# RWKV-7 recurrence stage: triangular inverse over four array quarters, half-width levels, state work moved into later levels

## What is computed

```python
def step(S, inp):                       # S: 64 x 64 per head
    r_t, w_t, k_t, v_t, a_t, b_t = inp
    sa = einsum('bhij,bhj->bhi', S, a_t)
    S = S * w_t[:, :, None, :] + sa[..., None] * b_t[:, :, None, :] + v_t[..., None] * k_t[:, :, None, :]
    return S, einsum('bhij,bhj->bhi', S, r_t)
S, ys = lax.scan(step, S0, xs)          # over 1024 tokens
```

## Time and profile before

| | us |
|---|---|
| median of 3 runs (1789.14 to 1791.79) | 1790.33 |
| the profiled execution's own time | 1789.6 |
| its span | 1787.8 |
| the recurrence stage in it, first activity to the store of the last state | about 468 to 732 |
| TensorE busy in the whole span | 1539.6 |
| VectorE busy | 668.1 |
| ScalarE busy | 371.5 |
| GpSimd busy | 211.5 |

### The profile page before, as it was taken

The page is one execution under the profiler, slowest core; times in us unless marked ns, Lnnn a source line. Parts: engine busy times, 40 slices in busy tenths (PEclk is TensorE's granted clock), DMA queues, the critical chain, the costliest instruction groups (busy, mean ns, idle before and its releaser), DMA issues. The chain is left out here.

```text
span 1787.8 us, 29869 instructions
## 1 busy us (share of the span) xinstructions
PE 1539.6 (86%) x11901; PEld 965.6 (54%) x11902; DVE 668.1 (37%) x1128; ACT 371.5 (21%) x813; POOL 211.5 (12%) x271
## 2 busy tenths in 40 slices
PE   7999999666899999546996699999499489999968
PEld 4666666454788888422442344444379344444433
DVE  1122560177255455481334311111478611111117
ACT  1232100266222322210001111111122111111111
POOL 3000000000322221210000111000500011110030
PEclk8999999877799999877998799999679789999989
DMA  6671110121000000005115688788501587867543
GB/s 178 151 306 48 26 46 0 39 67 25 2 4 4 4 4 4 8 0 156 36 38 185 241 287 294 279 283 261 202 22 61 177 289 275 304 240 254 188 172 148
DMA packets 138477, 237.23 MB, mean 133 GB/s; under 512 B 21570, under 2 KB 101427, under 8 KB 138090
## 3 DMA queue, kind: packets, MB, share of 16 engines
q1 hardware_dynamic: 114834, 151.01, 26.7%
q0 software_dynamic: 16912, 60.52, 9.2%
q10 hardware_dynamic: 6624, 24.12, 3.3%
HBM read 178.95 MB, written 58.21 MB: 133 GB/s over the span
## 5 line engine op out<-in xcount | busy, mean ns | idle before, releaser
L2094 PE MATMUL ex_pb<-ew_w_gate_up,ex_xT 128*128 x736 | 329.3, 601 | 6.1 <-DVE ex_xT L2139 2.3
L298 PE MATMUL pj_pb<-pj_xT,pj_w 128*128 128x348 f32 (+3 forms) x960 | 284.2, 457 | 0.4 <-ACT pj_xT L322 0.4
L298 PEld LDWEIGHTS pj_pb<-pj_xT,pj_w 128*128 128x128 f32 (+1 forms) x960 | 179.7, 187 | 102.7 <-issue 2.7
L2094 PEld LDWEIGHTS ex_pb<-ew_w_gate_up,ex_xT 128*128 128x128 f32 x736 | 137.7, 192 | 164.8 <-issue 163.8
L2077 PE MATMUL ex_pb<-ew_w_down,ex_hiddenT 128*128 x368 | 165.7, 593 | 3.4 <-ACT ex_hiddenT L2164 3.4
L2287 DVE TENSOR_TENSOR ex_hidden<-ex_hidden,ex_pb 128x256 f32<-128x256 f32 x46 | 19.4, 421 | 324.0 <-ACT ex_hidden L2159 324.0
L2077 PEld LDWEIGHTS ex_pb<-ew_w_down,ex_hiddenT 128*128 128x128 f32 x368 | 66.3, 190 | 69.9 <-issue 69.9
L1826 PE MATMUL mo_pb<-mo_w,minus_kk_then_y 128*128 128x512 f32 (+1 forms) x144 | 66.6, 617 | 20.8 <-DMA mo_w<-in_w_out 20.8
L2282 DVE COPY ex_y_rows<-ex_pb 128x512 f32<-128x512 f32 x46 | 31.8, 692 | 134.5 <-PE ex_pb L2077 134.5
L430 DVE SCALAR_TENSOR_TENSOR mixed<-pj_pb,v_mu,mixed 128x347 f32<-128x347 f32 (+3 forms) x42 | 24.0, 572 | 147.8 <-ACT mixed L372 147.7
L1826 PE MATMUL mo_pb<-mo_w,projected_qkv 128*128 128x512 f32 (+1 forms) x144 | 66.1, 614 | 7.3 <-DMA mo_w<-in_w_out 7.3
(11 more groups left out here) (428 smaller groups left out, 2292.6 us busy)
## 6 DMA issues: line engine op xcount, KB each, us to landing
ew_w_gate_up<-in_w_ex_gate SPq DMA_DIRECT2D x32, 1024.0 KB, 7.8
ew_w_gate_up<-in_w_ex_up SPq DMA_DIRECT2D x32, 1024.0 KB, 10.5
ew_w_down<-in_w_ex_down SPq DMA_DIRECT2D x32, 1024.0 KB, 13.1
scratch_slots_out<-ex_y_rows ACTq DMA_DIRECT2D x46, 512.0 KB, 5.2
scratch_slots_out<-pj_tmp POOLq DMA_DIRECT2D x4, 4096.0 KB, 15.9
scratch_x_stored<-x_rows SPq DMA_DIRECT2D x16, 512.0 KB
pj_w<-in_w_in SPq DMA_DIRECT2D x7, 1024.0 KB, 9.5
minus_kk_then_y<-in_x_prompt SPq DMA_DIRECT2D x8, 512.0 KB, 5.5
```

What stands on the lines that cost most here:

```text
L298: last = nc.tensor.matmul(product(at)[:, 0:tn], w[:, s % NW, k, c0:c0 + mrows], xT[:, k, x0:x0 + tn], start=(k == 0), stop=(k == KD - 1))
L2094: last = mm(pb[:, 2 + u, :], xT[:, u, k, :], w[:, k, :], start=(k == 0), stop=(k == KD - 1))
```

## The change

It rewrites `rwkv_chunks` and the masks it needs. What is computed, the tiles, the chunks and the number of levels stay.

- Quarters: for odd heads X (not XT) and Z live on the other half of the partitions (`to = fr(ch ^ par)`), and each group of products goes t, par, ch in turn, so that consecutive matmuls fall in all four quarters. The level products go to banks 6 and 7 (both Z and X), the transposes to 0 and 1.
- The product with r, the keys by a, and the output too go over four quarters; the output is now 32 matmuls of 64 x 64 instead of 16 of 128 x 128 columns.
- Both triangles (b a^T and a b^T) are made by TensorE (`triangles`), 32 matmuls instead of 16, so that XT of level 0 is masked directly; the GpSimd step that made X (L1052) and the VectorE step of L1270 fall away, and one VectorE step adds the identity.
- Half-width levels: a level changes only half of the columns, so Z, the addition to XT, the transposes of levels 1 to 4 and the copies of X use 32 columns per matrix.
- VectorE and ScalarE take both parities in one instruction.
- XT and RT have two buffers. The triangles of tile n+1 are made at the end of tile n, before the product with the values.
- State work of tile n-1 is spread over the levels of tile n: `state_by_w` at levels 0 and 2, `state_terms` after them, `state_update` in levels 1 and 3, `output` in level 4.
- RT holds only the diagonal blocks; the memset of RT at the start falls away.

TensorE's new parts and order:

```diff
+            def triangles(n):
+                pe.wait_ge(q["ft"], 2 * n + 1)
+                if n:
+                    pe.wait_ge(q["xc"], NLEV * n)
+                for t in range(4):
+                    for at, lhs, rhs in ((0, B, A), (256, A, B)):
+                        for par in range(2):
+                            for ch in range(2):
+                                cc = slice(P * n + CH * ch, P * n + CH * ch + CH)
+                                last = mm(pb[fr(ch), par, at + CH * t:at + CH * t + CH], lhs[fr(par), t, cc],
+                                          rhs[fr(par), t, cc], start=True, stop=True)
...
+            def transposed(n, lev):
...
+                                last = mm(grouped(pb[to, par, P * t:P * t + HALF], lev - 1), XT[cc, n % 2, par, t, :],
+                                          half_of(ident[cc, cc], lev - 1, 0), start=True, stop=True)
...
+            def level_z(n, lev):
+                if lev:
+                    pe.wait_ge(q["xe"], NLEV * n + lev)
+                    if n and lev in (1, 3):
+                        pe.wait_ge(q["uc"], 2 * (n - 1) + (lev + 1) // 2)
...
+                for t in range(4):
+                    for par in range(2):
+                        for ch in range(2):
+                            cc, to = fr(ch), fr(ch ^ par)
+                            last = mm(grouped(pb[to, 6 + par, P * t:P * t + HALF], lev), Lm[cc, par, t, :],
+                                      half_of(XT[cc, n % 2, par, t, :], lev, 1), start=True, stop=True)
+                last.then_inc(q["z"], 1)
+            def level_x(n, lev):
+                pe.wait_ge(q["zc"], NLEV * n + lev + 1)
+                if n and lev in (0, 2):
+                    state_by_w(n - 1, lev // 2)
+                pe.wait_ge(q["xc"], NLEV * n + lev + 1)
+                for t in range(4):
+                    for par in range(2):
+                        for ch in range(2):
+                            cc, to = fr(ch ^ par), fr(ch)
+                            last = mm(pb[to, 6 + par, P * t:P * t + HALF], X[cc, par, t, :], Z[cc, par, t, :],
+                                      start=True, stop=True)
...
+            triangles(0)
+            for n in range(NT):
+                transposed(n, 0)
+                level_z(n, 0)
+                by_r(n)
+                level_x(n, 0)
+                if n:
+                    state_terms(n - 1, 0)
+                level_z(n, 1)
+                transposed(n, 1)
+                if n:
+                    state_update(n - 1, 0)
+                keys_by_a(n)
+                level_x(n, 1)
+                level_z(n, 2)
+                transposed(n, 2)
+                level_x(n, 2)
+                if n:
+                    state_terms(n - 1, 1)
+                level_z(n, 3)
+                transposed(n, 3)
+                if n:
+                    state_update(n - 1, 1)
+                token_rows(n, 0)
+                level_x(n, 3)
+                token_rows(n, 1)
+                level_z(n, 4)
+                transposed(n, 4)
+                if n:
+                    output(n - 1)
+                token_rows(n, 2)
+                level_x(n, 4)
+                token_rows(n, 3)
+                if n + 1 < NT:
+                    triangles(n + 1)
+                values(n)
+                inverse_applied(n)
```

VectorE's order, and the widths of its steps:

```diff
+                tt(xt, up, four("lev0T"), ALU.mult).then_inc(q["x0"], 1)
+                dve.wait_ge(q["x0"], n + 1)
+                tt(flat(xt), flat(xt), eight("eye"), ALU.add).then_inc(q["xe0"], 1)
+                tt(Lm[:, :, :, :], low, four("low"), ALU.mult).then_inc(q["lc"], 1)
...
+            def take_z(n, lev):
+                dve.wait_ge(q["z"], NLEV * n + lev + 1)
+                tt(flat(Z[:, :, :, :]), level_out(6), eight(f"lev{lev + 1}T"), ALU.mult).then_inc(q["zc"], 1)
+            def take_x(n, lev):
+                dve.wait_ge(q["x"], NLEV * n + lev + 1)
+                new = halves_of(XT[:, n % 2, :, :, :], lev, 1)
+                tt(new, new, level_out_grouped(6, lev), ALU.add).then_inc(q["xe"], 1)
...
+            for n in range(NT):
+                take_triangles(n)
+                take_z(n, 0)
+                take_by_r(n, 0)
+                take_by_r(n, 1)
+                take_x(n, 0)
+                if n:
+                    take_u(n - 1, 0)
+                take_z(n, 1)
+                if n:
+                    take_state(n - 1, 0)
+                take_x(n, 1)
+                take_z(n, 2)
+                take_keys(n)
+                take_x(n, 2)
+                if n:
+                    take_u(n - 1, 1)
+                take_z(n, 3)
+                if n:
+                    take_state(n - 1, 1)
+                take_x(n, 3)
+                take_z(n, 4)
+                take_x(n, 4)
```

More of the change, by code:

```diff
@@ L1044, in scaled @@
                 last.then_inc(q["hat"], 1)
-            for z in (ST[:, 0, :, :], RT[:, :, :, :, :]):
-                nc.gpsimd.memset(z, 0.0).then_inc(q["start"], 1)
-            scaled(0)
+            nc.gpsimd.memset(ST[:, 0, :, :], 0.0).then_inc(q["start"], 1)
             for n in range(NT):
[L1051 to L1055, removed]
+                scaled(n)
         @block.tensor
@@ new lines, in level_x @@
+            def level_x(n, lev):
[3 more added lines that the diff above has]
+                pe.wait_ge(q["xc"], NLEV * n + lev + 1)
+                for t in range(4):
+                    for par in range(2):
+                        for ch in range(2):
+                            cc, to = fr(ch ^ par), fr(ch)
+                            last = mm(pb[to, 6 + par, P * t:P * t + HALF], X[cc, par, t, :], Z[cc, par, t, :],
+                                      start=True, stop=True)
+                last.then_inc(q["x"], 1)
@@ new lines, in token_rows @@
+            def token_rows(n, j):
+                src = (bh[:, :, :], kh[:, :, :], A[:, :, tile_cols(n)], pr[:, 8:12, tile_cols(n)])[j]
+                if j < 2:
+                    pe.wait_ge(q["mc"], n + 1)
+                    if n and j:
+                        pe.wait_ge(q["sc"], 2 * n)
+                    pe.wait_ge(q["hat"], n + 1)
+                else:
+                    pe.wait_ge(q["tc"], 4 * n + j - 1)
+                for t in range(4):
+                    last = nc.tensor.transpose(pb[:, 4 + j % 2, P * t:P * t + P], src[:, t, :], ident[:, :])
+                last.then_inc(q["tr"], 1)
@@ L1118, in output @@
             def output(n):
+                pe.wait_ge(q["sc"], 2 * n + 2)
                 for t in range(4):
-                    for par in range(2):
-                        hc = hcol(par, t)
-                        o = pb[fr(par), 3, P * t:P * t + P]
-                        mm(o, U[:, hc:hc + HD], RT[:, par, 0, t, :], start=False, stop=False)
-                        last = mm(o, tok[:, 3, hc:hc + HD], RT[:, par, 1, t, :], start=False, stop=(t == 3))
-                last.then_inc(q["y"], 1)
@@ new lines, in output @@
+                    for k in range(2):
+                        for ch in range(2):
+                            for par in range(2):
+                                tr, hc = fr(ch), hcol(par, t)
+                                lhs = U[tr, hc:hc + HD] if k == 0 else tok[tr, 3, hc:hc + HD]
+                                last = mm(pb[fr(par), 3 - ch, 256 + CH * t:256 + CH * t + CH], lhs,
+                                          RT[tr, n % 2, par, k, t, :], start=False, stop=(t == 3 and k == 1))
@@ new lines, in output, with values @@
+                last.then_inc(q["y"], 1)
+            def values(n):
+                pe.wait_ge(q["tc"], 4 * n + 4)
+                pe.wait_ge(q["mc"], n + 1)
+                for h in range(HA):
+                    for ch in range(2):
+                        cc = fr(ch)
+                        last = mm(pb[cc, 4, HD * h:HD * h + HD], MT[cc, h % 2, h // 2, :], tok[cc, 3, HD * h:HD * h + HD],
+                                  start=True, stop=True)
+                last.then_inc(q["mv"], 1)
@@ L1331, in _ @@
+                take_z(n, 4)
+                take_x(n, 4)
+            for ch in range(2):
+                take_u(NT - 1, ch)
+                take_state(NT - 1, ch)
         @block.sync
```

339 lines of the change are left out of this document (141 added, 198 removed).

## The result

| | before | after |
|---|---|---|
| median of 4 runs | 1789.74 (1787.13 to 1791.79) | 1776.05 (1773.95 to 1778.33) |
| span of the profiled execution | 1787.8 | 1772.0 |
| mean granted clock of TensorE, whole and in the stage | 0.913, 0.98 | 0.897, 0.87 |

The ratio is 0.992, 95% interval 0.9905 to 0.9935: faster by 14 us, where 66 had been forecast. The time lies outside the range given.

The account below looks back on a forecast made before the run. The recurrence was taken as bound by TensorE's own program. Seven steady tiles at 22.5 instead of 31.3 us (61.7), first tile 3.6 and last 0.9 made 66 us off the median 1790.3: 1724, range 1706 to 1744.

Parts of the forecast that it names:

- TensorE's issue time per tile: Recurrence: groups of 32 instructions over four quarters at 0.47 us instead of 0.93; together 19.0 us of the 31.28.
- the forecast 22.5: Steady tile of the recurrence after the change: 22.5 us, 8.8 less than 31.3; seven such tiles give 61.7.
- The walk of waits: One tile followed through levels and engine hops: 22.5 us, with TensorE pauses before Z groups ended by VectorE, 2.5 to 3.5.
- Rival 2: Recurrence: more waiting, strided masks and adds 0.50 and 0.75, groups 0.52; 24.6 us per tile, 1741; chance 0.15.
- rival 4: Recurrence, now with pauses, falls to 1.2 GHz: 38.1 us per tile, 1851; chance 0.02.
- Half width on TensorE: Level groups with 32 columns: no gain on TensorE taken, 0.45 to 0.47 us a group; pays on VectorE alone.
- rival 1: Level groups: half width counts on TensorE, groups of 0.27 us, 20.5 per tile, 1707; chance 0.12.
- The rule on shared banks: Skill rule: row tiles cannot share a PSUM bank simultaneously; Z and X groups would stay at 0.93 us.
- rival 3: Crossed quarters do not run side by side: groups stay at 0.93, 32.2 us per tile, about 1801; chance 0.03.
- The sum: Whole gain: 61.7 for seven steady tiles, 3.6 first tile, 0.9 last tile, 66 us.
- the terms written for the first tile: Start 472.3, triangles 1.9, hop and masks 2.4, tile 19.5, low clock 1.2: ends 497.1 against 500.7, 3.6 gained.
- The last tile with its tail: End of the stage: 0.9 gained without triangles to make, tail counted 0; last store near 662 instead of 728.

Follow-up runs that it names:

- the streams: Changed kernel plus, after the stage's last output, 1024 wait-free MATMUL instructions over four quarters, then 1024 over two; one run, 1833.16 us.
- 9: Kernel of 7 with 64 moving columns instead of 32 in its Z and X groups; 1743.45 us, ratio 0.9754 against the kernel before.
- 4: Changed kernel with 64 moving columns instead of 32 in the level groups, same instructions and order; 1771.53 us, ratio 0.9894 against the kernel before.
- 3: Changed kernel with three quarters of the transposes of levels 1 to 4 left out; 1758.56 us, ratio 0.9817 against the kernel before.
- 6: Changed kernel with level groups ordered parity by parity, two quarters taking turns; 1783.9 us, ratio 0.9959 against the kernel before.
- 7: Changed kernel with four full 128 x 128 transposes for 16 small ones per level, 280 instructions fewer per tile; 1751.2 us, ratio 0.9787.
- 8: Changed kernel with four 128 x 128 x 512 products ahead of the first tile's triangles; 1772.39 us, ratio 0.9886 against the kernel before.
- 11: Kernel of 9 with the four products of 8 ahead of the first triangles; 1743.35 us, ratio 0.9727 against the kernel before.

## Why the prediction was wrong

By its own steps:

- **"TensorE's issue time per tile" is the step that failed.** Each group was priced as in the earlier trace rows, 32 instructions in 0.47 us, and that price is right: 0.46 to 0.49 after. But it is a price for a short burst out of instructions already loaded. The sum of 19.0 us asks for 256 instructions in 2.6 us, and even the forecast 22.5 for 256 in 3.0; the streams show that they come in 3.5 to 3.7. The floor for a tile is therefore 7.4 blocks, 26 to 27.5 us, and the tiles at full clock took 26.6 and 28.0. The kernel before, with blocks 4.5 us apart, stayed above this limit and showed 0.2 us of idle by "issue". Its count could have been set against the new time, 887 + 884 instructions in 31.27 us and more than that in 22.5, as a warning; its price stood in no row.
- **The walk of waits** was right in kind: TensorE's pauses ended by VectorE are 12.3 us in the stage, 1.5 per tile, less than the 2.5 to 3.5 forecast. That the holes before a block cover some of them is an inference; in 9, where such holes are few, the pauses are 19.7 us, 2.5 per tile. Rival 2 named the sign that was seen (the same groups, a period over 24) but its cause, slower masks and additions, was not there: 420 ns for an addition of 256, as before.
- **The clock, rival 4, was given 2 in 100** on the ground that TensorE would stay busy for 20 of 22.5 us without a long pause. It was busy for 22 to 27 of 27 to 32 us, and still 64 us of the stage ran at 1.2 GHz; the whole first tile did, for which 1.2 us had been set down. The ground did not hold: 4 was busy for less (181 of 245 us) than the change (197) and had a clock of 0.97, not 0.87. The one thing that its edit changes is the width of what moves. The price was small because the blocks hid most of it: full width gave back 4.5 us in the changed kernel, and 10 where fewer instructions had moved the limit away.
- **Half width on TensorE**: nothing was gained, as taken from the earlier trace rows, and the groups at 32 and 64 columns (0.60 and 0.62 us) show it; rival 1 is out. That it costs clock was not thought of.
- **The rule on shared banks** did no harm: groups with both row halves in one bank ran at 0.46 to 0.49, so rival 3 is out.
- **The sum.** Tile 7 began at 674.08 where the walk puts it at 632.1 (497.1 and six times 22.5; the terms written for the first tile give 497.3): 42.0 us late. 7.3 of them are the first tile, at half clock nearly throughout, and 34.7 are six tiles at 28.3 instead of 22.5. Of the 5.8 per tile the two tiles at full clock show 4.1 and 5.5 without any help of the clock, 3.4 and 4.9 of it idle by "issue". The last tile with its tail adds 6 more: the last store is at 710.16 and not near 662.

```profile
708.88 0.63 PE L1302 MATMUL rc_pb<-k_ident,rc_ST 128*64 128x128 f32 x4
...
710.16 0.64 SPq L1404 DMA_DIRECT2D out_rwkv_prompt<-rc_MV  x1
```

What stays open: why the clock is lower with narrow products than with wide ones and more idle time; what takes the 3.6 us of a block, since in the streams each 16 KB packet moves within one slice of 0.2 us; and how much of the 39 to 44 ns of a met wait is the wait and how much the fetching of it.

## What to carry to other kernels

Before pricing a TensorE program by its groups, divide the new time by its instructions, matmuls and weight loads both. Here nothing ran for long below 14 ns each; a plan that comes out under that has to remove instructions, not only speed them up, even by wider and individually slower ones. And when a change narrows what moves through the array, forecast its clock as a case of its own.

## What was not expected of the hardware

- Blocks of 256 instructions followed each other every 3.47 to 3.75 us when they were all that TensorE waited for, with holes of 1.4 to 1.7 us where four quarters used them up.
- Over four quarters 32 matmuls with their loads pass in 0.47 us, 15 ns from start to start in the mean, and 128 in 2.1. The Trainium skill, TensorE: Matmul & The Clock Gate, section "Wait — 56ns, not 53.3ns?", has starts never under about 25 ns apart; these rows do not agree.
- 64 waits that were already met held TensorE up for 2.5 us in the changed kernel and 2.8 in the one before, 39 and 44 ns each; with them the time at half clock grew from 64 to 218 us and from 10 to 117.
- 32 moving columns instead of 64 took 14 us of half clock to 64 us, with the same instructions in the same order. The other runs with 32 columns had 41 to 72 us (3, 6, 7 and 8), the two others with 64 had 14 and 3 (9 and 11).
